# Fox-GLA encoder block on one core: six of sixteen k blocks of the first projection group multiplied as whole fp32 products

## Chip, cores and metric

One core of a Trainium2 chip runs the whole program. The metric is the device time in microseconds; lower is better. All tensors are float32. The kernel gets more accuracy out of TensorE than its fast fp32r format has by splitting each operand into a high part (the value rounded to fp32r) and a low part (what is left), and adding three products.

## The reference, cut to what matters

One layer with a token mixer and an MLP. Only its first part bears on this change: the shift and the scale of the first normalisation come from the conditioning vector `c` through `w_ada`, and the modulated `h` is multiplied by the columns of `w_in`.

```
mod = (c_act @ w_ada[i] + b_ada[i])[:, None, :]
shift_m, scale_m, gate_m, shift_f, scale_f, gate_f = jnp.split(mod, N_MOD, axis=-1)
h = rmsnorm(x, g_pre_mix[i]) * (1.0 + scale_m) + shift_m
...
proj = h @ w_in
fq, fk, fv, ff, gq, gk, gv, ga, gr = jnp.split(proj, IN_OFFSETS, axis=-1)
...
x = x + gate_m * rmsnorm(y, g_post_mix[i])
h = rmsnorm(x, g_pre_mlp[i]) * (1.0 + scale_f) + shift_f
y = squared_relu_mlp(h, w_mlp_in[i], w_mlp_out[i])
```

`x` is 512 x 2048, `w_ada` 2048 x 12288 and `w_in` 2048 x 6168.

## The kernel before

**Stages.** After a start (rows of `x` normalised, transposed into `xn_t`) the projection runs in eight groups of six 128-column tiles (`group_steps`, from L743), the first four for the attention heads and the last four for the linear-attention heads; the work of the heads of group r is threaded between the products of group r+1. Then follow the output projection, the MLP's input products and the MLP's output products. This change touches the first group (r = 0, `first=True`) and no other.

**One group.** Its depth of 2048 is cut into KT = 16 k blocks of 128. Two k blocks make a weight unit (units 0 to 7 of 128 x 1536 elements, 768 KB), which lands in `w_raw`, is rounded by ScalarE into `w_hi` (`split_hi`, `first_hi`) and subtracted by VectorE into `w_lo` (`split_lo`, `first_lo`). There are two slots of each, by the unit's parity. For each k block TensorE makes 6 tiles x 3 products of 128 x 128 by 128 x 512 into six PSUM banks (`split_mm`, L731: high by high, high by low, low by high), all 16 k blocks adding into the same banks.

**The first group** differs from the others in that the moving operand isn't there yet. It is made k block by k block: ScalarE writes `in_tmp` = scale * xn_t + shift (L1271) and rounds it to `in_hi` (L1274), and VectorE subtracts to `in_lo` (`modulated_lo`, L1817). `in_lo` and `in_tmp` are the same bytes. The scale and shift of four k blocks (a "block" of the VectorE program; there are four, 0 to 3) come from eight items of `w_ada` of 1 MB each (`load_am`, items 0 to 31, four buffers): VectorE multiplies and adds each item's two halves into `am_acc` (`add_am`, L1800 and L1802), TensorE then sums over partitions by 16 tiny matmuls (`start_slot`, L922, in TensorE's queue ahead of the block's products), and VectorE makes the columns `mod_a`, `mod_b` (`mod_columns_m`, L1832 to L1835) for which ScalarE waits. TensorE's program also has 16 narrow steps (`misc_step`, 40 columns of weights `wm_raw`, split in the same way), put at k blocks 5 to 15 by `MISC_AT`: k 5 to 9 have two each (steps 0, 1; 2, 3; 4, 5; 6, 7; 8, 9), k 10 to 15 have one.

**VectorE's order** for block b: mod columns; `w_lo` of unit 2b; `in_lo` of k 4b and 4b+1; (blocks 1 and 2) `wm_lo`; items; `w_lo` of unit 2b+1; `in_lo` of k 4b+2; one item; `in_lo` of k 4b+3; more items. In all these are nine items in block 0 (8 to 16), eight in block 1 (17 to 24), seven in block 2 (25 to 31) and none in block 3.

**SyncE's queue** issues all these transfers in one order: items in sequence, each when the item four before it has been used (`am_used`); small transfers of `wm_raw` behind items 9 to 24; unit 2 behind item 13, unit 3 behind item 17, unit 4 behind 21, unit 5 behind 25, unit 6 behind 29 and unit 7 behind 31. A unit of weights waits until the unit two before it has been split by both engines (`slot_free`, L473).

Of the kernel before, what the change touches and what calls it, by code (L numbers as in the profile page):

```python
# [45 lines left out]
def build_block(nc, x, c, w_ada, b_ada, g_pre_mix, g_post_mix, w_in, b_fgate, w_gla_a2, b_gla_a2,  # L46
# [64 lines left out]
    with ExitStack() as ctx:  # L111
# [261 lines left out]
        o_rstd = sem("o_rstd")  # L373
        o_ready = sem("o_ready")

        def arrived_group(r, mm):
            return 16 * GROUP_DMAS * (r * (MM_G // 2) + mm // 2 + 1)

# [90 lines left out]
        def _(sp):  # L469
# [2 lines left out]
                sp.wait_ge(hi_done, m - 1)  # L472
                sp.wait_ge(lo_done, m - 1)  # L473

            def load_fox(r, mm, wait=True):
                if wait:
                    slot_free(r * MM_G + mm)
                dst = group_view(w_raw[mm % 2])
                for k in range(2):
                    src = w_in_t[:, 2 * mm + k, 0:3 * FOX_WIDTH].rearrange("p (s n) -> p s n", s=3)  # L480
                    to = dst[:, k, :].rearrange("p (s n) -> p s n", s=3)
                    for part in (slice(0, 2), slice(2, 3)):
                        sp.dma_start(to[:, part, :], src[:, part, bass.ds(r * 2 * P, 2 * P)])\
                            .then_inc(w_in_s[mm % 2], 16)
# [109 lines left out]
            for n in range(9, 32):  # L594
                load_am(n)
                if n < 25:
                    load_wm(n - 9)
                if n == 25:
                    sp.dma_start(b_fg[32:40, :], b_fgate.rearrange("o h -> h o")).then_inc(bfg_in, 16)
                if n >= 13 and n % 4 == 1:  # L600
                    load_fox(0, (n - 5) // 4)
            load_fox(0, MM_G - 1)


            def load_cumb(f):
# [124 lines left out]
        def _(pe):  # L730
            def split_mm(dst, a, b, start, stop, onto=False):  # L731

                pe.matmul(dst, a[0], b[0], start=start, stop=False, skip_group_check=onto)  # L733
                pe.matmul(dst, a[0], b[1], start=False, stop=False, skip_group_check=onto)  # L734
                return pe.matmul(dst, a[1], b[0], start=False, stop=stop, skip_group_check=onto)  # L735

            def group_steps(r, first, slot, misc_step=None):

                for k in range(KT):
                    s, m = (k // 2) % 2, r * MM_G + k // 2  # L740
                    hi, lo = group_view(w_hi[s])[:, k % 2, :], group_view(w_lo[s])[:, k % 2, :]
                    if first:
                        slot(2 * k)  # L743
                    if k % 2 == 0:
                        pe.wait_ge(hi_done, m + 1)
                        pe.wait_ge(lo_done, m + 1)
                    if first:
                        pe.wait_ge(mod_lo, k + 1)
                        for n in MISC_AT[k]:
                            misc_step(n)  # L750
                    for b in range(TILES):
                        if k == 0 and not first:

                            pe.wait_ge((ev_act, ev_dve)[b % 2], r * 3 - 2 + b // 2)
                        cols = slice(b * P, b * P + P)
                        last = split_mm(bank[b][:, :], (hi[:, cols], lo[:, cols]),
                                        (in_hi[:, k, :], in_lo[:, k, :]), k == 0, k == KT - 1)
                        if k == KT - 1 and b < TILES - 1:
                            last.then_inc(tile_sum, 1)
                        if b == TILES - 1 and k % 2:  # L760
                            last.then_inc(w_used, 1)
                        if not first and b == 2:
                            slot(2 * k)
                    if not first:
                        slot(2 * k + 1)
# [161 lines left out]
            def misc_step(k):  # L927

                if k % 8 == 0:
                    pe.wait_ge(wm_hid, k // 8 + 1)  # L930
                    pe.wait_ge(wm_lod, k // 8 + 1)
                last = split_mm(BB[0:40, :], (wm_hi[:, k, :], wm_lo[:, k, :]), (in_hi[:, k, :], in_lo[:, k, :]),
                                k == 0, k == KT - 1)
                if k == KT - 1:
                    last.then_inc(misc_sum, 1)

# [2 lines left out]
            def fox_slots(f):  # L939
                def slot(s):  # L940
                    fox_slot(s, f)
                    if s == 30:
                        pe.wait_ge(fox_max, 8 * f + 8)
                        f_columns(f)
                return slot


            def first_fox_slot(s):
                if s == 0:
                    pe.wait_ge(cum_ready, 1)  # L950
                    for t in range(TB):
                        last = pe.transpose(BA[:, t * FOX_HEADS:(t + 1) * FOX_HEADS],
                                            f_z[32:40, t * P:t * P + P], ident[32:40, 32:40])
                    last.then_inc(cumq_tr, 1)
                if s == 1:
                    pe.wait_ge(cumq_ready, 1)
                fox_slots(0)(s)

            group_steps(1, False, first_fox_slot)
# [167 lines left out]
        def _(act):  # L1127
            def split_hi(m, arrived, n, view=slice(0, 2048)):

                act.wait_ge(w_in_s[n], arrived)  # L1130
                act.wait_ge(w_used, m - 1)
                act.activation(w_hi[n][:, view], w_raw[n][:, view], ACT.Copy).then_inc(hi_done, 1)  # L1132
# [132 lines left out]
            def first_hi(m):  # L1265
                act.wait_ge(w_in_s[m], arrived_group(0, m))
                act.activation(w_hi[m][:, NARROW], w_raw[m][:, NARROW], ACT.Copy).then_inc(hi_done, 1)
# [9 lines left out]
            for k in range(KT):  # L1277
                if k in (4, 8):
                    part = slice(2 * k - 8, 2 * k)
                    act.wait_ge(wm_in[k // 4 - 1], 256)  # L1280
                    act.activation(wm_hi[:, part, :], wm_raw[:, part, :], ACT.Copy).then_inc(wm_hid, 1)
                modulate(k)
                if k == 1:
                    first_hi(1)
                if k % 2 and 3 <= k < KT - 1:
                    mm = (k + 1) // 2
                    split_hi(mm, arrived_group(0, mm), mm % 2, NARROW)

            split_hi(MM_G, arrived_group(1, 0), 0, NARROW)
            act.wait_ge(fz_abs, 1)  # L1290
# [264 lines left out]
        def _(dve):  # L1555
# [259 lines left out]
            def modulated_lo(k, n):  # L1815
                dve.wait_ge(mod_hi, n + 1)
                dve.tensor_tensor(in_lo[:, k, :], in_tmp[:, k, :], in_hi[:, k, :].bitcast(F32),  # L1817
                                  ALU.subtract).then_inc(mod_lo, 1)

            def first_lo(m):  # L1820
                dve.wait_ge(hi_done, m + 1)
                dve.tensor_tensor(w_lo[m][:, NARROW], w_raw[m][:, NARROW], w_hi[m][:, NARROW].bitcast(F32),
                                  ALU.subtract).then_inc(lo_done, 1)

            def mod_columns_m(block):
                k = slice(4 * block, 4 * block + 4)

# [8 lines left out]

            for n in range(2, 8):
                add_am(n)
            for block in range(KT // 4):
                mod_columns_m(block)  # L1840
                if block == 0:
                    first_lo(0)
                else:
                    split_lo(2 * block, 0, NARROW)
                n = 8 * block + 8
                more = block < KT // 4 - 1
                modulated_lo(4 * block, 4 * block)
                modulated_lo(4 * block + 1, 4 * block + 1)
                if block == 0:
                    add_am(n)  # L1850
                if block in (1, 2):
                    part = slice(8 * block - 8, 8 * block)
                    dve.wait_ge(wm_hid, block)
                    dve.tensor_tensor(wm_lo[:, part, :], wm_raw[:, part, :], wm_hi[:, part, :].bitcast(F32), ALU.subtract)\
                        .then_inc(wm_lod, 1)
                if more:
                    add_am(n + 1)
                    add_am(n + 2)
                if block == 0:
                    first_lo(1)  # L1860
                else:
                    split_lo(2 * block + 1, 1, NARROW)
                modulated_lo(4 * block + 2, 4 * block + 2)
                if more:
                    add_am(n + 3)
                modulated_lo(4 * block + 3, 4 * block + 3)
                if more:
                    for i in range(4, 9 if block < KT // 4 - 2 else 8):
                        add_am(n + i)
            dve.wait_ge(am_used, 32)  # L1870

            split_lo(MM_G, 0, NARROW)
            dve.wait_ge(misc_sum, 1)
# [487 lines left out]
```

## Time and profile before

| what | value |
| --- | --- |
| median of 3 runs | 2239.73 us (2239.48 to 2239.76) |
| time of the profiled execution | 2241.82 us |
| its span in the trace | 2240.0 us |
| mean granted TensorE clock | 0.989 |
| TensorE busy | 2163.1 us, 97% of the span |
| first group's products in the trace | 44.93 to 154.94 us |

The span is the time from the first to the last instruction. The profiled execution took 1.82 us more than its span and 2.09 us more than the median of the runs. The first group is 5% of the span. PE is TensorE's matmuls, PEld its weight loads, DVE is VectorE, ACT ScalarE, POOL GpSimd and SP SyncE. A matmul's duration in a row reaches past the start of the next, because matmuls are pipelined; what one costs is read from start to start. In the trace's rows a split product's two kinds are named by L733, L734 and L735.

### The profile page before, as it was taken

How to read it: one execution, taken by the hardware profiler on the slowest of the kernel's cores; microseconds unless marked ns; L12 is line 12 of the kernel's file. 1: busy time of each engine (PE TensorE's matmuls, PEld its weight loads, DVE VectorE, ACT ScalarE, POOL GpSimd, SP SyncE). 2: the span in 40 equal slices, each digit the busy share in tenths (PEclk: the TensorE clock that was granted, in tenths of full speed). 3: DMA queues.
4: the chain of work that ended last, by engine and by line, in shares of the span. 5: the costliest groups of instructions: out<-in, count | busy, mean ns of one | idle time of the engine just before them, and what ended most of it. 6: DMA issues, size and time to landing. Idle time of an engine off the chain costs nothing.

```text
span 2240.0 us, 26539 instructions
## 1 busy us (share of the span) xinstructions
PE 2163.1 (97%) x9847; PEld 1769.0 (79%) x9847; DVE 1510.3 (67%) x1467; ACT 868.8 (39%) x1094; POOL 379.2 (17%) x209
## 2 busy tenths in 40 slices
PE   4799999999999999999999999999999999999996
PEld 3577888887777788888888888888878888888885
DVE  6967666666767634655445544543698989898998
ACT  6333333331334223534334335334444444343443
POOL 1000000000000000100000000000034545463645
PEclk9899999999999999999999999999999999999998
DMA  9946555653553352566656646756355664567663
GB/s 366 347 158 228 189 172 165 226 156 101 185 164 116 112 214 76 192 221 225 202 194 217 223 170 205 246 183 202 132 196 179 239 232 166 191 232 245 236 232 143
DMA packets 262306, 441.16 MB, mean 197 GB/s; under 512 B 18156, under 2 KB 110512, under 8 KB 256184
## 3 DMA queue, kind: packets, MB, share of 16 engines
q1 hardware_dynamic: 261376, 435.45, 57.8%
q10 hardware_dynamic: 824, 4.27, 0.5%
q8 instruction: 70, 1.15, 0.2%
q14 instruction: 36, 0.29, 0.0%
HBM read 379.88 MB, written 59.79 MB: 196 GB/s over the span
## 4 chain that ended last, share of the span: by engine, by line
PE 78%; issue 8%; DVE 6%; DMA 2%; ACT 1%; DVEq 1%; POOL 1%; SPq 1%; POOLq 0%; ACTq 0%
PE pair L733 25%; PE pair L735 25%; PE pair L734 25%; DVE am_acc L1800 3%; DMA w_raw<-in_w_in 1%; PE pair L830 1%; DMA am_item<-in_w_ada 1%; DVE v_op L2067 1%; PE pair L804 1%; DVEq L1799 1%; POOL v_raw L2319 0%; PE pair L922 0%; PE pair L870 0%; PE pair L821 0%; PE pair L879 0%
## 5 line engine op out<-in xcount | busy, mean ns | idle before, releaser
L733 PE MATMUL pair<-in_hi,w_hi 128*128 128x512 f32 (+1 forms) x1824 | 730.1, 400 | 12.0 <-DVE in_lo L1817 6.5
L735 PE MATMUL pair<-in_hi,w_lo 128*128 128x512 f32 (+1 forms) x1824 | 707.3, 388 | 0.0
L734 PE MATMUL pair<-in_lo,w_hi 128*128 128x512 f32 (+1 forms) x1824 | 706.3, 387 | 0.0
L1560 DVE TENSOR_TENSOR w_lo<-w_raw,w_hi 128x2048 fp32r<-128x2048 f32 (+1 forms) x142 | 294.7, 2075 | 407.2 <-ACT w_hi L1132 406.7
L1132 ACT ACTIVATE w_hi<-w_raw 128x2048 fp32r<-128x2048 f32 (+1 forms) x142 | 244.9, 1725 | 466.3 <-PE pair L735 416.6
L733 PEld LDWEIGHTS pair<-in_hi,w_hi 128*128 128x128 f32 x1824 | 344.6, 189 | 92.1 <-issue 22.1
L735 PEld LDWEIGHTS pair<-in_hi,w_lo 128*128 128x128 f32 x1824 | 343.8, 188 | 71.6
L734 PEld LDWEIGHTS pair<-in_lo,w_hi 128*128 128x128 f32 x1824 | 345.0, 189 | 69.0 <-issue 2.6
L733 PE MATMUL pair<-v_op,hid_r 128*128 128x512 f32 x896 | 349.1, 390 | 2.1 <-issue 0.8
L735 PE MATMUL pair<-v_op,hid_r 128*128 128x512 f32 x896 | 348.6, 389 | 0.0
L734 PE MATMUL pair<-v_op,hid_r 128*128 128x512 f32 x896 | 348.6, 389 | 0.0
L2067 DVE TENSOR_TENSOR v_op<-v_raw,v_op 128x1024 fp32r<-128x1024 f32 x192 | 302.3, 1595 | 64.6 <-ACT v_op L1537 63.5
L1537 ACT ACTIVATE v_op<-v_raw 128x1024 fp32r<-128x1024 f32 x192 | 203.3, 1061 | 287.0 <-PE pair L735 269.0
L2310 POOL TENSOR_TENSOR v_sum<-v_raw,v_raw 128x512 f32<-128x512 f32 x60 | 149.2, 2515 | 363.3 <-DVE v_raw L2082 363.3
L733 PEld LDWEIGHTS pair<-v_op,hid_r 128*128 128x128 f32 x896 | 168.2, 188 | 39.0 <-issue 3.2
L735 PEld LDWEIGHTS pair<-v_op,hid_r 128*128 128x128 f32 x896 | 168.2, 188 | 35.0
L734 PEld LDWEIGHTS pair<-v_op,hid_r 128*128 128x128 f32 x896 | 168.2, 188 | 34.7
L2319 POOL TENSOR_TENSOR v_raw<-v_raw,v_sum 128x512 f32<-128x512 f32 x60 | 135.4, 2288 | 18.4 <-DVE v_op L2067 18.4
L2237 POOL TENSOR_TENSOR ada<-ada,c_act 128x2048 f32<-128x2048 f32 x8 | 30.4, 3804 | 592.3 <-DMA ada<-in_w_ada 555.0
L2117 DVE TENSOR_TENSOR y_t<-pair,y_t 128x1024 f32<-128x1024 f32 x104 | 124.9, 1214 | 0.3 <-PE pair L735 0.3
L733 PE MATMUL pair<-w_hi,in_hi 128*128 128x512 f32 x256 | 101.2, 395 | 0.0
L734 PE MATMUL pair<-w_lo,in_hi 128*128 128x512 f32 x256 | 99.7, 389 | 0.0
(205 smaller groups left out, 1886.0 us busy)
## 6 DMA issues: line engine op xcount, KB each, us to landing
w_raw<-in_w_mlp_in SPq DMA_DIRECT2D x64, 1024.0 KB, 5.3
v_raw<-in_w_mlp_out SPq DMA_DIRECT2D x128, 512.0 KB, 5.0
hid_r<-hid_scratch SPq DMA_DIRECT2D x112, 512.0 KB, 6.2
hid_scratch<-hid_r SPq DMA_DIRECT2D x28, 1792.0 KB, 8.3
am_item<-in_w_ada SPq DMA_DIRECT2D x64, 512.0 KB, 7.2
w_raw<-in_w_in SPq DMA_DIRECT2D x128, 256.0 KB, 3.6
af_item<-in_w_ada SPq DMA_DIRECT2D x64, 512.0 KB, 4.5
w_raw<-in_w_in SPq DMA_DIRECT2D x128, 128.0 KB, 3.6
```

What stands on the lines that cost most here:

```text
L733: pe.matmul(dst, a[0], b[0], start=start, stop=False, skip_group_check=onto)
L734: pe.matmul(dst, a[0], b[1], start=False, stop=False, skip_group_check=onto)
L735: return pe.matmul(dst, a[1], b[0], start=False, stop=stop, skip_group_check=onto)
L1132: act.activation(w_hi[n][:, view], w_raw[n][:, view], ACT.Copy).then_inc(hi_done, 1)
L1537: act.activation(v_op[i % 4][:, 0, :], raw_of(u, p)[:, h, :], ACT.Copy).then_inc(v_hi, 1)
L1560: dve.tensor_tensor(w_lo[n][:, view], w_raw[n][:, view], w_hi[n][:, view].bitcast(F32), ALU.subtract)\
L1800: last = dve.scalar_tensor_tensor(total, item, c_k, total, ALU.mult, ALU.add)
L2067: dve.tensor_tensor(v_op[i % 4][:, 1, :], raw_of(u, p)[:, h, :], v_op[i % 4][:, 0, :].bitcast(F32), ALU.subtract).then_inc(v_lo, 1)
L2117: return dve.tensor_tensor(dst, src[:, :, :], dst, ALU.add)
L2237: pool.tensor_tensor(unit[:, :, :], unit[:, :, :], c_act[:, :].rearrange("p (k o) -> p k o", o=1).to_broadcast([P, KT, P]), ALU.mult)\
L2310: last = pool.tensor_tensor(v_sum[:, h, cols], v_raw[q[B22]][:, h, cols], v_raw[q[B11]][:, h, cols], ALU.add)
L2319: last = pool.tensor_tensor(b21, b21, v_sum[:, h, cols], ALU.subtract)
```

## The change

For the weight units 1, 3 and 5 of the first group (k blocks 2, 3, 6, 7, 10 and 11), TensorE multiplies `w_raw` by `in_tmp` in one fp32 `pe.matmul` per tile instead of three products of parts; the same holds for the narrow steps of those k numbers (`wm_raw` by `in_tmp`). These units are split neither by ScalarE nor by VectorE. TensorE waits for the arrival of the raw unit and for `mod_tmp` instead of for the splits. As `in_lo` overwrites `in_tmp`, VectorE makes the `in_lo` of these six k blocks after the items are done and after unit 5 has been used (`w_used` of 6). A transfer into a slot whose last unit was a whole one waits for TensorE's use of that unit: unit 3 for unit 1, unit 5 for unit 3, unit 7 for unit 5. The counts of `hi_done` and `lo_done` are made up by 3 when unit 6 is split.

```diff
--- before.py
+++ after.py
@@ -373,6 +373,16 @@
         o_rstd = sem("o_rstd")
         o_ready = sem("o_ready")
 
+        WHOLE = (1, 3, 5)
+
+        def whole(k):
+            return k // 2 in WHOLE
+
+        LO_ORDER = [k for k in range(KT) if not whole(k)] + [k for k in range(KT) if whole(k)]
+
+        def splits(m):
+            return m + 1 if m > max(WHOLE) else sum(u not in WHOLE for u in range(m + 1))
+
         def arrived_group(r, mm):
             return 16 * GROUP_DMAS * (r * (MM_G // 2) + mm // 2 + 1)
 
@@ -472,8 +482,13 @@
                 sp.wait_ge(hi_done, m - 1)
                 sp.wait_ge(lo_done, m - 1)
 
-            def load_fox(r, mm, wait=True):
-                if wait:
+            def load_fox(r, mm, wait=True, first=False):
+                if wait and first and mm - 2 in WHOLE:
+                    sp.wait_ge(w_used, mm - 1)
+                elif wait and first:
+                    sp.wait_ge(hi_done, splits(mm - 2))
+                    sp.wait_ge(lo_done, splits(mm - 2))
+                elif wait:
                     slot_free(r * MM_G + mm)
                 dst = group_view(w_raw[mm % 2])
                 for k in range(2):
@@ -598,8 +613,8 @@
                 if n == 25:
                     sp.dma_start(b_fg[32:40, :], b_fgate.rearrange("o h -> h o")).then_inc(bfg_in, 16)
                 if n >= 13 and n % 4 == 1:
-                    load_fox(0, (n - 5) // 4)
-            load_fox(0, MM_G - 1)
+                    load_fox(0, (n - 5) // 4, first=True)
+            load_fox(0, MM_G - 1, first=True)
 
 
             def load_cumb(f):
@@ -741,11 +756,18 @@
                     hi, lo = group_view(w_hi[s])[:, k % 2, :], group_view(w_lo[s])[:, k % 2, :]
                     if first:
                         slot(2 * k)
-                    if k % 2 == 0:
-                        pe.wait_ge(hi_done, m + 1)
-                        pe.wait_ge(lo_done, m + 1)
+                    raw = group_view(w_raw[s])[:, k % 2, :]
+                    by_parts = not (first and whole(k))
+                    if k % 2 == 0 and not by_parts:
+                        pe.wait_ge(w_in_s[s], arrived_group(0, m))
+                    elif k % 2 == 0:
+                        pe.wait_ge(hi_done, splits(m) if first else m + 1)
+                        pe.wait_ge(lo_done, splits(m) if first else m + 1)
                     if first:
-                        pe.wait_ge(mod_lo, k + 1)
+                        if by_parts:
+                            pe.wait_ge(mod_lo, LO_ORDER.index(k) + 1)
+                        else:
+                            pe.wait_ge(mod_tmp, k + 1)
                         for n in MISC_AT[k]:
                             misc_step(n)
                     for b in range(TILES):
@@ -753,8 +775,11 @@
 
                             pe.wait_ge((ev_act, ev_dve)[b % 2], r * 3 - 2 + b // 2)
                         cols = slice(b * P, b * P + P)
-                        last = split_mm(bank[b][:, :], (hi[:, cols], lo[:, cols]),
-                                        (in_hi[:, k, :], in_lo[:, k, :]), k == 0, k == KT - 1)
+                        if by_parts:
+                            last = split_mm(bank[b][:, :], (hi[:, cols], lo[:, cols]),
+                                            (in_hi[:, k, :], in_lo[:, k, :]), k == 0, k == KT - 1)
+                        else:
+                            last = pe.matmul(bank[b][:, :], raw[:, cols], in_tmp[:, k, :], start=False, stop=False)
                         if k == KT - 1 and b < TILES - 1:
                             last.then_inc(tile_sum, 1)
                         if b == TILES - 1 and k % 2:
@@ -929,8 +954,11 @@
                 if k % 8 == 0:
                     pe.wait_ge(wm_hid, k // 8 + 1)
                     pe.wait_ge(wm_lod, k // 8 + 1)
-                last = split_mm(BB[0:40, :], (wm_hi[:, k, :], wm_lo[:, k, :]), (in_hi[:, k, :], in_lo[:, k, :]),
-                                k == 0, k == KT - 1)
+                if whole(k):
+                    last = pe.matmul(BB[0:40, :], wm_raw[:, k, :], in_tmp[:, k, :], start=False, stop=False)
+                else:
+                    last = split_mm(BB[0:40, :], (wm_hi[:, k, :], wm_lo[:, k, :]), (in_hi[:, k, :], in_lo[:, k, :]),
+                                    k == 0, k == KT - 1)
                 if k == KT - 1:
                     last.then_inc(misc_sum, 1)
 
@@ -954,6 +982,7 @@
                     last.then_inc(cumq_tr, 1)
                 if s == 1:
                     pe.wait_ge(cumq_ready, 1)
+                    pe.wait_ge(mod_lo, KT)
                 fox_slots(0)(s)
 
             group_steps(1, False, first_fox_slot)
@@ -1280,11 +1309,11 @@
                     act.wait_ge(wm_in[k // 4 - 1], 256)
                     act.activation(wm_hi[:, part, :], wm_raw[:, part, :], ACT.Copy).then_inc(wm_hid, 1)
                 modulate(k)
-                if k == 1:
-                    first_hi(1)
-                if k % 2 and 3 <= k < KT - 1:
-                    mm = (k + 1) // 2
+                mm = (k + 1) // 2
+                if k % 2 and 3 <= k < KT - 1 and mm not in WHOLE:
                     split_hi(mm, arrived_group(0, mm), mm % 2, NARROW)
+                    if mm == max(WHOLE) + 1:
+                        act.sem_inc(hi_done, len(WHOLE))
 
             split_hi(MM_G, arrived_group(1, 0), 0, NARROW)
             act.wait_ge(fz_abs, 1)
@@ -1817,11 +1846,6 @@
                 dve.tensor_tensor(in_lo[:, k, :], in_tmp[:, k, :], in_hi[:, k, :].bitcast(F32),
                                   ALU.subtract).then_inc(mod_lo, 1)
 
-            def first_lo(m):
-                dve.wait_ge(hi_done, m + 1)
-                dve.tensor_tensor(w_lo[m][:, NARROW], w_raw[m][:, NARROW], w_hi[m][:, NARROW].bitcast(F32),
-                                  ALU.subtract).then_inc(lo_done, 1)
-
             def mod_columns_m(block):
                 k = slice(4 * block, 4 * block + 4)
 
@@ -1836,12 +1860,18 @@
 
             for n in range(2, 8):
                 add_am(n)
+            def lo_first(m):
+                dve.wait_ge(hi_done, splits(m))
+                dve.tensor_tensor(w_lo[m % 2][:, NARROW], w_raw[m % 2][:, NARROW], w_hi[m % 2][:, NARROW].bitcast(F32),
+                                  ALU.subtract).then_inc(lo_done, 1)
+                if m == max(WHOLE) + 1:
+                    dve.sem_inc(lo_done, len(WHOLE))
+
             for block in range(KT // 4):
                 mod_columns_m(block)
-                if block == 0:
-                    first_lo(0)
-                else:
-                    split_lo(2 * block, 0, NARROW)
+                if block:
+                    dve.wait_ge(w_used, 2 * block - 1)
+                lo_first(2 * block)
                 n = 8 * block + 8
                 more = block < KT // 4 - 1
                 modulated_lo(4 * block, 4 * block)
@@ -1856,18 +1886,19 @@
                 if more:
                     add_am(n + 1)
                     add_am(n + 2)
-                if block == 0:
-                    first_lo(1)
+                if not more:
+                    split_lo(2 * block + 1, 1, NARROW)
+                    modulated_lo(4 * block + 2, 4 * block + 2)
+                    modulated_lo(4 * block + 3, 4 * block + 3)
                 else:
-                    split_lo(2 * block + 1, 1, NARROW)
-                modulated_lo(4 * block + 2, 4 * block + 2)
-                if more:
                     add_am(n + 3)
-                modulated_lo(4 * block + 3, 4 * block + 3)
                 if more:
                     for i in range(4, 9 if block < KT // 4 - 2 else 8):
                         add_am(n + i)
             dve.wait_ge(am_used, 32)
+            dve.wait_ge(w_used, max(WHOLE) + 1)
+            for k in LO_ORDER[-2 * len(WHOLE):]:
+                modulated_lo(k, k)
 
             split_lo(MM_G, 0, NARROW)
             dve.wait_ge(misc_sum, 1)
```

## Rows read from the trace of the kernel before

**Rows 1.** The page, first part: busy time, share and instructions of each engine.
```profile
PE 2163.1 (97%) x9847; PEld 1769.0 (79%) x9847; DVE 1510.3 (67%) x1467; ACT 868.8 (39%) x1094; POOL 379.2 (17%) x209
```

**Rows 2.** Windows by stage, first group; PE: stretch, length, busy, clock, DMA share, GB/s.
```profile
44.93:64.48 19.55, 18.89 (x72) 0.89 1.08 369
64.48:70.23 5.75, 0.00 (x0) 0.95 1.07 364
...
76.76:98.96 22.20, 22.20 (x90) 0.93 0.99 327
...
105.30:128.37 23.07, 23.07 (x90) 0.88 0.83 289
128.37:133.83 5.46, 2.10 (x17) 0.75 0.00 0
133.83:154.94 21.11, 21.11 (x84) 0.90 0.39 125
```

**Rows 3.** Waits from 40 to 160 us: in total, times, the longest.
```profile
PE pair L733 <- DVE in_lo L1817: 12.4, 5, 3.0
...
PE pair L922 <- DVE am_acc L1800: 7.4, 3, 5.8
```

**Rows 4.** Timeline, VectorE, first block and the start of the second: start, length.
```profile
53.52 1.75 DVE L1822 TENSOR_TENSOR w_lo<-w_raw,w_hi 128x1536 fp32r<-128x1536 f32 x1
...
58.54 0.69 DVE L1817 TENSOR_TENSOR in_lo<-in_tmp,in_hi 128x512 fp32r<-128x512 f32 x1
59.32 10.86 DVE L1800 SCALAR_TENSOR_TENSOR am_acc<-am_item,c_act,am_acc 128x1024 f32<-128x1024 f32 x8
70.09 0.74 DVE L1802 TENSOR_SCALAR am_acc<-am_item,c_act 128x1024 f32<-128x1024 f32 x1
70.91 1.28 DVE L1800 SCALAR_TENSOR_TENSOR am_acc<-am_item,c_act,am_acc 128x1024 f32<-128x1024 f32 x1
73.84 0.16 DVE L1832 TENSOR_TENSOR mod_b<-pair,cols_a 128x4 f32<-128x4 f32 x1 [1.64 <-PE pair L922]
```

**Rows 5.** Timeline, TensorE: an fp32 product of a later group between split ones.
```profile
189.25 1.02 PE L804 MATMUL pair<-grp 128*128 128x512 f32 x2
...
190.34 0.40 PE L734 MATMUL pair<-in_lo,w_hi 128*128 128x512 f32 x1
```

**Rows 6.** Timeline, TensorE: the first rows of two stretches that lie 18 products apart.
```profile
119.47 0.39 PE L733 MATMUL pair<-in_hi,w_hi 128*128 128x512 f32 x1
...
123.55 0.39 PE L733 MATMUL pair<-in_hi,wm_hi 128*40 128x512 f32 x1
```

**Rows 7.** Timeline, TensorE: the column sums ahead of the second, third and fourth block.
```profile
70.23 3.57 PE L922 MATMUL pair<-ones,am_acc 128*128 128x1 f32 x16 [5.76 <-DVE am_acc L1800]
...
100.40 1.95 PE L922 MATMUL pair<-ones,am_acc 128*128 128x1 f32 x16 [1.28 <-DVE am_acc L1800]
...
128.93 1.95 PE L922 MATMUL pair<-ones,am_acc 128*128 128x1 f32 x16 [0.41 <-DVE am_acc L1800]
```

**Rows 8.** Windows of all engines: stretch, length, busy of five engines, clock, DMA share, GB/s.
```profile
44.00:64.00 20.00, 18.42 (x71) 14.84 (x72) 18.44 (x18) 6.90 (x9) 0.00 (x0) 0.87 1.08 369
...
80.00:82.00 2.00, 2.00 (x11) 1.60 (x10) 1.91 (x2) 1.27 (x2) 0.00 (x0) 1.00 0.53 170
```

**Rows 9.** The tile am_item, the two transfers issued at 58.6 us: from issue to landing.
```profile
L570 SPq DMA_DIRECT2D am_item<-in_w_ada x2: 379/426/472, 58.6 to 59.1; - x2
...
DMA to landing us min/median/max: 5.7/6.5/7.3
```

**Rows 10.** Timeline, SyncE's queue: when transfers were issued.
```profile
66.72 2.22 SPq L483 DMA_DIRECT2D w_raw<-in_w_in  x4
...
94.90 0.89 SPq L570 DMA_DIRECT2D am_item<-in_w_ada  x2
...
96.34 1.94 SPq L483 DMA_DIRECT2D w_raw<-in_w_in  x4
98.33 12.16 SPq L570 DMA_DIRECT2D am_item<-in_w_ada  x8
```

## What the change is predicted to do

> **What bounds the kernel now.** I read the page first: TensorE is busy for 97% of the span [rows 1], so nearly all the rest of the program moves one for one with the moment at which the first group ends. The question is the first group alone. The windows by stage [rows 2] show it as four blocks of TensorE work with gaps: 44.93 to 64.48, 76.76 to 98.96, 105.30 to 128.37 and 133.83 to 154.94 us. The first gap is 12.3 us long, the second 6.3, the third 5.5. The waits say who ends them: VectorE's item sums ahead of the column sums, 7.4 us in all, and then `in_lo`, 12.4 us in five waits [rows 3]. Four of these five are the fixed turnaround behind the column sums, about 2.95 us each: mod columns, one `w_lo`, one `in_lo`. From the start of warm column sums to the first product it is 105.30 - 100.40 = 4.90 and 133.83 - 128.93 = 4.90 us [rows 2, 7]. Outside that turnaround TensorE waited 5.75 us for VectorE ahead of block 1 (64.48 to 70.23), about 1.4 ahead of block 2 (98.96 to 100.40) and about 0.5 ahead of block 3 (128.37 to 128.93). That is the reader's main point: **VectorE leads the first gap only; in the other two TensorE follows it by about one microsecond**.
>
> **VectorE.** The change takes from each of blocks 0, 1 and 2 one `w_lo` and two `in_lo` [rows 4]. A `w_lo` shows 1.75 us and an `in_lo` 0.69; from start to start they are a little shorter (58.54 to 59.32 with the drain is 0.78, a `w_lo` about 1.67). So 1.67 + 0.69 + 0.78 = 3.15 us a block, 9.4 in all. The six `in_lo` come back behind the items, 6 x 0.69 = 4.1 us, in block 3. There VectorE has only two `w_lo` and four `in_lo` to make, some 6 us, while TensorE computes for 21.1 us [rows 2]; they are first read in group 1. I cost them at nothing; without that cover they would cost 4.1 us.
>
> **TensorE.** Three split products come one after another each 0.227 us: 18 of them lie in 123.55 - 119.47 = 4.08 us [rows 6]. So a split step is 0.68 us. The nearest row for an fp32 product of the same shape is L804 in a later group: it is recorded as two instructions, starts at 189.25, and the second split product behind it starts at 190.34; less one split product of 0.23 that leaves 0.86 us [rows 5]. A whole step thus costs 0.18 us more. That price isn't shown for a long row of such products. The bound below is two instructions at a split product's pace, 0.45; the one above is the 1.02 us that the row shows for the pair. I take 0.86, as it is a reading from start to start of this very operation. How many steps: 12 tiles in each of blocks 0, 1, 2, and narrow steps 2 and 3 (k 6), 6 and 7 (k 8), 10 and 11. Block 0 gains 12 x 0.18 = 2.1 us of work, block 1 14 x 0.18 = 2.5, block 2 16 x 0.18 = 2.85; 7.5 us in all. In block 0 the wait of about 1 us for `in_lo` and `w_lo` inside the block goes away, so block 0 ends at 64.5 + 2.1 - 1.0 = 65.5.
>
> The Trainium skill's page "TensorE: Matmul & The Clock Gate", section "Wait — 56ns, not 53.3ns?", gives 215.7 ns from one warm 512-column matmul to the next, and "FP8 and Floating Point Precision", section "TensorE Precision Notes", gives true fp32 four passes. By these pages a whole step would be 0.86 us and a split one 0.65, the 42 steps would cost 9.1 us and the result would be 1.2 us later than mine. The trace's 0.227 [rows 6] decides, since it is this kernel's own.
>
> **Block 1's start.** Does VectorE's 3.15 us arrive? The transfers say: not all. From 44 to 64 us the DMA engines are full (share 1.08, 369 GB/s) [rows 8], so what must land by a given moment is fixed by bytes, not by when it is asked for. The item whose last sum ends block 0's demand (item 15) was issued at 58.65 and 59.1 us, its last half landed 7.3 us later, at 66.4 [rows 9]. VectorE began it at about 67.5 and was done at 70.18 [rows 4]. So it can be done at 66.4 + 2.73 = 69.1 at the earliest: **1.05 us of gain, not 3.15**. Item 16 (0.74 + 1.28) stands before the mod columns as now. The column sums were slow here, 3.57 us against 1.95 [rows 7], nearly twice as long, as at 1.2 instead of 2.4 GHz; the clock of the gap ahead of them is 0.95 on the mean [rows 2], so it fell late in it. With a shorter idle (65.5 to 69.2) it may be granted longer, for up to 1.6 us more; I don't count on it. Block 1 starts at 76.76 - 1.05 = 75.7.
>
> **From there TensorE leads.** Block 1: 22.20 + 2.5 = 24.7 us, to 100.4. VectorE needs to be ready for block 2 by then: it starts its items 1.05 us earlier and has no `w_lo` and `in_lo` between them, so its last sum, now at 100.2, comes at about 96.2. Column sums and turnaround 4.9: block 2 starts at 105.3, as before. Block 2: 23.07 + 2.85 = 25.9, to 131.2. Again 4.9 and some 0.1: block 3 starts at 136.2 against 133.83. Block 3 has no whole step. **The first group ends 2.3 us later.** Its pieces against before: +5.35 of work in blocks 1 and 2, -1.05 at block 1's start, -1.9 of waits for VectorE used up (1.4 and 0.5).
>
> **SyncE's queue.** The new waits on `w_used` stand in one queue with the items. Unit 3 now waits for the end of block 0 (65.5), which is earlier than it was issued (66.72) [rows 10], and nothing is late. Unit 5 waits for the end of block 1, 100.4, where it was issued at 96.34; behind it are items 26 to 31. Item 26 was issued at 98.33 and is now at 102.3. Items 24 and 25 are ahead of the stall. VectorE uses item 25 at 106.6 to 109.3 and then one each 2.73 us, item 28 lands about 112.5 (three items of 1.05 MB at 369 GB/s, 2.85 us each, behind the unit), so the last sum comes at about 125.7, and TensorE asks for it at 131.2: 5.5 us of cover. Unit 7 waits for 131.2 instead of 118; it lands by about 136.5, and is first wanted by TensorE at about 148. ScalarE loses three roundings of 1.5 us, off the path.
>
> **Sum.** The profiled execution took 2241.82 us; by this it becomes 2244.1. The median stood 2.09 us below it, so the median becomes 2239.73 + 2.3 = 2242.0. About 0.2% (4.5 us) is what a measurement of this kernel can tell from no change, so this counts as none.
>
> **Rivals.**
> 1. *VectorE's full gain reaches block 1.* If the transfers give way, block 1 starts at 72.0 (3.15 us from VectorE, 1.6 from warm column sums). Then 96.7, 101.6, 127.5, 132.4: 1.4 us faster, 2238.3. Against it: a share of 1.08 [rows 8] and only 0.53 once VectorE had let the queue run dry. The Trainium skill's "DMA: Bandwidth & Descriptors", section "Bandwidth", states 425 GB/s for large loads where the row has 369; by that rate this rival would hold. Chance 0.12.
> 2. *Whole steps are cheap* (a run of them overlaps so that each costs no more than a split step's 0.68). Then only the transfers and VectorE count: blocks 1, 2 and 3 keep their gain, 1.05, then 3.15 more each at best less the 1.4 and 0.5 us that TensorE has to give. 1.05 + 1.4 + 0.5 = 3 us; with full gain at block 1 as in the first rival 6.6 us faster, 2233 to 2236.7. Against it: two instructions of 0.43 in L804's row [rows 5]. Chance 0.06.
> 3. *Slower: whole steps are dear.* A run of fp32 products costs more than a lone one, up to the pair's 1.02 us. 42 x 0.34 = 14.3 us of work instead of 7.5, of which block 0's hides in the gap: 30 x 0.16 = 4.8 on top of 2.3, 2246.8. It passes 0.2% from 0.93 us a step on. For it: nobody has shown twelve in a row; against it: weight loads of 0.19 us fit under 0.43. Chance 0.09.
> 4. *Slower: unit 5's wait starves VectorE.* It decides once item 31's sum is over 5.5 us later than I find; beyond that each microsecond counts, and 2244.5 to 2248 would come out. Chance 0.05.
> Each block also starts at 1.2 GHz: mean clock 0.93 in block 1 and 0.88 in block 2 [rows 2], so, at half the clock, stretches of (1 - 0.93) x 2 x 22.2 = 3.1 and 5.5 us, worth 1.2 us between the best and the worst in each block. That was hidden by VectorE before and isn't now.
>
> **Numbers.** My case has 0.68. The range takes in the first rival and product prices to 0.92: 2238.0 to 2245.0. Faster by over 0.2% is the second rival's upper part, 0.05; slower is rivals 3 and 4 with the unlucky end of my own case, 0.15; the same 0.80.
>
> **What the changed profile would show.** Whole products as pairs 0.86 us apart; block 0 ending at 65.5; column sums ahead of block 1 at 69.1; no wait of L922 for `am_acc` ahead of blocks 2 and 3, with VectorE idle before the mod columns; block 2 starting at 105.3, block 3 at 136.2. I am wrong if L922 still waits for VectorE ahead of block 2, if block 1 starts before 74 us, or if whole steps aren't within 0.85 to 0.9.

## The result, and the profile after

The changed kernel takes 2243.89 us (median of 22 runs, 2241.24 to 2245.94) against 2240.06 us for the kernel before in the same series (22 runs). The ratio is 1.0015, 95% interval 1.0009 to 1.0021: 3.4 us slower, 2.0 to 4.7 (the two medians lie 3.8 us apart). The forecast was 2242.0 us, 2.3 slower, in a range of 2238.0 to 2245.0. The measured time lies in that range and the loss is below the 4.5 us that the forecast took for the least it could tell, but it is clear of zero. The profiled execution took 2243.09 us with a span of 2241.2 us.

Windows by stage of the changed kernel, first group; the columns are those of [rows 2]:

```profile
45.03:65.69 20.66, 20.66 (x60) 0.90 1.08 369
65.69:68.81 3.12, 0.01 (x1) 1.00 1.07 362
...
74.65:100.40 25.75, 25.75 (x76) 0.90 0.95 327
...
105.29:131.95 26.66, 26.66 (x74) 0.90 0.73 264
131.95:136.81 4.86, 1.90 (x17) 0.76 0.56 162
136.81:158.11 21.30, 21.30 (x84) 0.89 0.39 124
```

Blocks 1 and 2 are longer than in [rows 2], by 3.6 us each; block 3, which has no whole step, is not. The wait ahead of block 1 has shrunk from 5.75 us to 3.12.

From the start of group 1 to the end the two profiled executions took 2083.4 us (before) and 2081.4 (changed); over all twelve profiles of this document it is 2081.1 to 2083.4. So single profiles show where the first group's time goes, but a difference of one or two microseconds in the whole is read from the medians: group 1 starts 3.2 us later here, while the two spans differ by only 1.2.

Waits of the changed kernel from 40 to 160 us, beside [rows 3]:

```profile
DVE mod_b L1856 <- PE pair L947: 13.0, 4, 5.6
...
DVE am_acc L1829 <- DMA am_item<-in_w_ada: 5.3, 6, 2.3
...
PE pair L947 <- DVE am_acc L1829: 3.1, 1, 3.1
```

The roles have turned. TensorE waits for the item sums once, ahead of block 1, instead of three times. VectorE waits 13.0 us for TensorE's column sums (7.2 before), and 5.3 us for the transfers, which it did not wait for in this stretch before.

Timeline of the changed kernel, TensorE, the column sums and whole steps up to block 2 (start, length), beside [rows 7]:

```profile
68.81 2.88 PE L947 MATMUL pair<-ones,am_acc 128*128 128x1 f32 x16 [3.12 <-DVE am_acc L1829]
74.65 0.77 PE L748 MATMUL pair<-in_hi,w_hi 128*128 128x512 f32 x1 [2.96 <-DVE in_lo L1846]
...
88.69 5.42 PE L782 MATMUL pair<-in_tmp,w_raw 128*128 128x512 f32 x12
...
95.34 5.32 PE L782 MATMUL pair<-in_tmp,w_raw 128*128 128x512 f32 x12
100.49 1.73 PE L947 MATMUL pair<-ones,am_acc 128*128 128x1 f32 x15
```

A row x12 is one k block: six products, recorded as two instructions each. From 95.34 to the sums at 100.49 it is 5.15 us for six, 0.86 us each. Block 0's twelve lie between 55.23 and 65.69, 0.87 each. Ahead of the sums at 100.49 there is no idle time.

Timeline of the changed kernel, VectorE: the item sums of block 0 and of block 2, beside [rows 4]:

```profile
54.23 8.13 DVE L1829 SCALAR_TENSOR_TENSOR am_acc<-am_item,c_act,am_acc 128x1024 f32<-128x1024 f32 x6 [0.52 <-issue]
63.26 2.64 DVE L1829 SCALAR_TENSOR_TENSOR am_acc<-am_item,c_act,am_acc 128x1024 f32<-128x1024 f32 x2 [0.90 <-DMA am_item<-in_w_ada]
66.12 2.64 DVE L1829 SCALAR_TENSOR_TENSOR am_acc<-am_item,c_act,am_acc 128x1024 f32<-128x1024 f32 x2 [0.21 <-DMA am_item<-in_w_ada]
...
109.74 10.86 DVE L1829 SCALAR_TENSOR_TENSOR am_acc<-am_item,c_act,am_acc 128x1024 f32<-128x1024 f32 x8 [0.16 <-DMA am_item<-in_w_ada]
122.90 5.38 DVE L1829 SCALAR_TENSOR_TENSOR am_acc<-am_item,c_act,am_acc 128x1024 f32<-128x1024 f32 x4 [2.31 <-DMA am_item<-in_w_ada]
133.89 0.16 DVE L1856 TENSOR_TENSOR mod_b<-pair,cols_a 128x4 f32<-128x4 f32 x1 [5.61 <-PE pair L947]
```

Items 14 and 15 (63.26, 66.12) are each begun when they land. In block 2 item 30 is begun when it lands, at 122.9, with item 31 right behind it. They are late, but VectorE ends them at 128.3, 3.7 us before TensorE ends block 2 (131.95). Its wait of 5.6 us is these 3.7 and the column sums.

Timeline of the changed kernel, SyncE's queue, the stall of unit 5, beside [rows 10]:

```profile
90.14 1.30 SPq L585 DMA_DIRECT2D am_item<-in_w_ada  x2
91.48 0.42 SPq L614 DMA_DIRECT2D b_fg<-in_b_fgate  x1
100.69 1.88 SPq L498 DMA_DIRECT2D w_raw<-in_w_in  x4
102.61 7.88 SPq L585 DMA_DIRECT2D am_item<-in_w_ada  x8
```

For 9 us nothing is issued. The forecast had unit 5 at 100.4 and item 26 at 102.3.

### The profile page after: what moved, and what is told of

Its sections match the earlier page's. It is cut to its first block, busy times and chain, and to the rows that moved or that the text cites. A ratio compares the mean times of both kernels' runs of the same rounds, so it can differ in the third digit from the quotient of the medians.

```text
span 2241.2 us, 26445 instructions
## 1 busy us (share of the span) xinstructions
PE 2170.7 (97%) x9805; PEld 1761.1 (79%) x9805; DVE 1506.4 (67%) x1464; ACT 864.9 (39%) x1091; POOL 378.4 (17%) x209
## 4 chain that ended last, share of the span: by engine, by line
PE 83%; issue 8%; DVE 3%; DMA 2%; POOL 1%; SPq 1%; ACT 1%; POOLq 0%; DVEq 0%; ACTq 0%
PE pair L748 26%; PE pair L750 26%; PE pair L749 26%; DMA am_item<-in_w_ada 1%; DVE am_acc L1829 1%; PE pair L782 1%; PE pair L855 1%; PE pair L829 1%; DVE v_op L2098 1%; PE pair L947 0%; DMA w_raw<-in_w_in 0%; POOL v_raw L2350 0%; PE pair L846 0%; PE pair L895 0%; PE pair L904 0%
## 5 line engine op out<-in xcount | busy, mean ns | idle before, releaser
L748 PE MATMUL pair<-in_hi,w_hi 128*128 128x512 f32 (+1 forms) x1788 | 716.2, 401 | 11.4 <-DVE in_lo L1846 5.9
L750 PE MATMUL pair<-in_hi,w_lo 128*128 128x512 f32 (+1 forms) x1788 | 693.4, 388 | 0.0
L749 PE MATMUL pair<-in_lo,w_hi 128*128 128x512 f32 (+1 forms) x1788 | 692.6, 387 | 0.0
L1589 DVE TENSOR_TENSOR w_lo<-w_raw,w_hi 128x2048 fp32r<-128x2048 f32 (+1 forms) x137 | 286.0, 2088 | 401.2 <-ACT w_hi L1161 400.6
L748 PEld LDWEIGHTS pair<-in_hi,w_hi 128*128 128x128 f32 x1788 | 337.9, 189 | 91.0 <-issue 22.5
L750 PEld LDWEIGHTS pair<-in_hi,w_lo 128*128 128x128 f32 x1788 | 337.2, 189 | 70.1
L749 PEld LDWEIGHTS pair<-in_lo,w_hi 128*128 128x128 f32 x1788 | 338.2, 189 | 67.5 <-issue 2.6
```

Source lines behind the costliest of these rows:

```text
L1589: dve.tensor_tensor(w_lo[n][:, view], w_raw[n][:, view], w_hi[n][:, view].bitcast(F32), ALU.subtract)\
```

## Experiments

All were run in five rounds beside the kernel before. The table holds, from each profile, the length of the column sums ahead of block 0, the start of those ahead of block 1, the starts of blocks 1, 2 and 3 and of group 1 (us), and the ratio of the times to the kernel before.

| kernel | sums 0, length | sums 1 | block 1 | block 2 | block 3 | group 1 | ratio (95% interval) |
| --- | --- | --- | --- | --- | --- | --- | --- |
| before | 3.31 | 70.23 | 76.76 | 105.30 | 133.83 | 156.63 | 1 |
| changed | 3.39 | 68.81 | 74.65 | 105.29 | 136.81 | 159.79 | 1.0015 (1.0009 to 1.0021) |
| unit 1 only | 3.46 | 69.03 | 75.27 | 103.82 | 132.35 | 155.70 | 0.9999 (0.9990 to 1.0008) |
| units 1, 3 | 2.20 | 69.00 | 75.52 | 106.43 | 134.96 | 157.86 | 1.0004 (0.9995 to 1.0013) |
| units 3, 5 | 2.98 | 69.85 | 76.38 | 105.78 | 137.24 | 160.19 | 1.0021 (1.0012 to 1.0030) |
| half columns | 1.92 | 69.36 | 75.89 | 102.78 | 129.14 | 152.28 | 0.9984 (0.9975 to 0.9993) |
| unit 5 later | 1.92 | 69.15 | 75.68 | 105.61 | 136.75 | 159.24 | 1.0018 (1.0009 to 1.0027) |
| unit 2 later | 1.92 | 66.79 | 73.44 | 104.09 | 135.57 | 158.52 | 1.0012 (1.0003 to 1.0021) |
| unit 1 only, unit 2 later | 1.92 | 66.85 | 73.47 | 102.08 | 131.65 | 154.88 | 0.9991 (0.9982 to 1.0000) |
| the same again | 1.92 | 66.76 | 73.38 | 102.33 | 131.56 | 155.12 | 0.9990 (0.9981 to 0.9999) |
| unit 1 only, unit 2 at 15 | 1.92 | 66.82 | 74.17 | 102.71 | 131.24 | 154.84 | 0.9996 (0.9987 to 1.0005) |
| before, unit 2 later | 1.92 | 69.10 | 75.64 | 104.18 | 132.73 | 155.42 | 1.0001 (0.9992 to 1.0010) |

**1. Only unit 1 whole.**

```diff
-        WHOLE = (1, 3, 5)
+        WHOLE = (1,)
```

with `split_lo` and the two `modulated_lo` back in the VectorE program for units not in `WHOLE`.

> Only unit 1 (block 0) is multiplied whole; units 3 and 5 are split again, with their in_lo in the old places. Theory (TensorE leads from block 1 on, so whole steps there are pure cost, and block 0's are hidden by the wait for the items): block 1 starts at 74.6 us as in the changed kernel, then VectorE leads again at its old pace: block 2 at 103.2, block 3 at 131.7, each 2.1 us earlier than before the change; the time 2.1 us below before, 5 us below the changed kernel. Rival (the new waits in SyncE's queue, not TensorE's work, cost the time): unit 3's wait is still there, so part of the loss stays and block 2 starts at 105 or later.

Blocks 2 and 3 start at 103.82 and 132.35: 1.5 us before the kernel before and 4.5 before the changed one at block 3. The rival, 105 or later at block 2, fell. These are the sums ahead of blocks 2 and 3 in the timeline of TensorE:

```profile
98.92 1.95 PE L947 MATMUL pair<-ones,am_acc 128*128 128x1 f32 x16
...
127.45 1.95 PE L947 MATMUL pair<-ones,am_acc 128*128 128x1 f32 x16 [1.44 <-DVE am_acc L1829]
```

Ahead of block 3 TensorE waits 1.44 us for VectorE again. Ahead of block 2 neither waits: VectorE's last sum ends at 98.86 and TensorE's last product at 98.88. The loss is gone, so it sits in units 3 and 5. But the expected 2.1 us of gain is not in the profile (1.5 us at blocks 2 and 3, 0.9 at group 1), and the time (between 2.2 us less and 1.8 more) can't tell 0.9 us from none. That part of the theory missed; see below.

**2. Units 1 and 3 whole** (`WHOLE = (1, 3)`).

> Units 1 and 3 are whole, unit 5 is split. Theory: blocks 0 and 1 as in the changed kernel (74.65, 105.3), block 2 back to about 23.5 us of TensorE work, 128.8. But the items behind unit 5's wait come late, and VectorE has 3.1 us of splits between them again, so it may lead: block 3 starts between 133.8 and 135.5 against 136.8 in the changed kernel; the time 0 to 1.7 us above before. Rival (whole steps cost nothing and the waits do): block 3 still at 136.8.

Block 3 at 134.96, inside what was expected, and the time 0.9 us above before (between 1.1 less and 2.9 more). Blocks 1 and 2 started 0.9 and 1.1 us later than expected. From the start of block 1 to that of block 3 it is 57.1 us with unit 1 alone, 59.4 here and 62.2 in the changed kernel: each of the two later units adds its part. VectorE did not lead again: the sums ahead of block 3 began at 130.17 without a wait.

**3. Units 3 and 5 whole** (`WHOLE = (3, 5)`, and `first_hi(1)` back in ScalarE's program).

> Units 3 and 5 whole, unit 1 split as before the change: the part of the change that the theory calls pure cost, alone. Theory: block 1 starts at 76.8 us as before, block 2 at 106.5 to 107.3, block 3 at 138 to 139, group 1 at 161 to 162, 4 to 5 us later than before; the time 4 to 5.5 us above before, above the changed kernel too. Rival (the parts share one gain on VectorE): block 2 no later than 105.3.

2.7 to 6.7 us slower than before. The marks are 0.4 to 0.8 us earlier than the expected ranges and block 2 came only 0.5 us behind the rival's 105.3, but the direction holds: without the gain at block 1 the two later units alone put group 1 at 160.19, later than all three do (159.79). The times of this kernel and of the changed one can't be told apart.

**4. Half the columns of the wide whole products.**

```diff
-                            last = pe.matmul(bank[b][:, :], raw[:, cols], in_tmp[:, k, :], start=False, stop=False)
+                            last = pe.matmul(bank[b][:, 0:256], raw[:, cols], in_tmp[:, k, 0:256], start=False, stop=False)
```

> The changed kernel with the second half of the columns left out of the 36 wide whole products (256 of 512), waits and order unchanged. Theory: a wide whole step costs 0.44 us instead of 0.87, 5.2 us less in each of blocks 0, 1 and 2. Block 1 starts at 74.65 unchanged; block 2 at about 101.8 (VectorE's items end at 96.9), block 3 at about 128; the time 8 to 9 us below the changed kernel, about 5 below before. Rival (TensorE's work doesn't lead): block 2 still at 105.3 and the time within 1 us of the changed kernel.

Windows of this kernel, TensorE, block 2 (21.12 us, where the changed kernel's has 26.66):

```profile
102.78:123.90 21.12, 21.11 (x74) 0.91 0.83 300
```

and its timeline, the sums that follow:

```profile
97.68 1.95 PE L947 MATMUL pair<-ones,am_acc 128*128 128x1 f32 x16 [1.66 <-DVE am_acc L1829]
...
124.23 1.95 PE L947 MATMUL pair<-ones,am_acc 128*128 128x1 f32 x16 [0.34 <-DVE am_acc L1829]
```

With about 5.5 us less work in a block, TensorE waits for VectorE again and block 3 starts 7.7 us before the changed kernel's; block 1's start is not earlier. TensorE's work is what led there. The gain stops where VectorE takes over, about 1 us sooner than expected: the time is 3.6 us below before (1.6 to 5.6) where about 5 was expected.

**5. Unit 5's load later in SyncE's queue.**

```diff
-                if n >= 13 and n % 4 == 1:
+                if n >= 13 and n % 4 == 1 and n != 25:
                     load_fox(0, (n - 5) // 4, first=True)
+                if n == 28:
+                    load_fox(0, 5, first=True)
```

> The changed kernel with unit 5's load put behind item 28 instead of item 25, so that its wait for w_used holds back no item that could go earlier. Theory (the stall in SyncE's queue is covered): items 26 to 28 are issued before 100 us, VectorE ends its items at 126 instead of 128.3 us, TensorE's blocks stay at 105.3 and 136.8, the time within 0.7 us of the changed kernel. Rival (the stall costs): block 3 starts 1 to 2 us earlier, and so the time.

Its VectorE sums all of block 2's items without a break, and then waits 1.9 us longer for TensorE than in the changed kernel (5.61):

```profile
107.26 19.07 DVE L1831 SCALAR_TENSOR_TENSOR am_acc<-am_item,c_act,am_acc 128x1024 f32<-128x1024 f32 x14
133.84 0.16 DVE L1858 TENSOR_TENSOR mod_b<-pair,cols_a 128x4 f32<-128x4 f32 x1 [7.51 <-PE pair L949]
```

Block 3 starts at 136.75 against 136.81. The stall in the queue costs nothing here.

**6. Unit 2's load behind item 16.**

```diff
-                if n >= 13 and n % 4 == 1:
+                if n >= 17 and n % 4 == 1:
                     load_fox(0, (n - 5) // 4, first=True)
+                if n == 16:
+                    load_fox(0, 2, first=True)
```

> The changed kernel with unit 2's load (768 KB, 2.1 us of the engines' time) put behind item 16 instead of item 13, where it is no longer ahead of items 14 and 15. Theory (full transfer engines, not VectorE, set when block 1 starts; in all four kernels run so far the column sums ahead of it began between 68.8 and 69.4 us, wherever block 0 began): VectorE no longer waits for items 14 and 15, the column sums begin at 67.6 to 68.0, and as TensorE leads from there the whole group ends 0.5 to 1.3 us earlier than in the changed kernel. Rival (VectorE sets it): still 68.8 or later.

The sums ahead of block 1 begin at 66.79, even earlier than expected. Timeline of this kernel, VectorE: ten item sums, those of items 14 and 15 among them, without a wait, and then a new one:

```profile
53.14 13.60 DVE L1831 SCALAR_TENSOR_TENSOR am_acc<-am_item,c_act,am_acc 128x1024 f32<-128x1024 f32 x10 [0.65 <-DMA am_item<-in_w_ada]
66.97 0.75 DVE L1833 TENSOR_SCALAR am_acc<-am_item,c_act 128x1024 f32<-128x1024 f32 x1 [0.23 <-DMA am_item<-in_w_ada]
...
70.94 1.76 DVE L1867 TENSOR_TENSOR w_lo<-w_raw,w_hi 128x1536 fp32r<-128x1536 f32 x1 [1.39 <-ACT w_hi L1163]
```

Unit 2 now comes late for its own split (1.39 us), so block 1 gains about 2.2 us on experiment 5's and not 3.6. Group 1 starts 0.7 us before experiment 5's and 1.3 before the changed kernel's. The time (0.7 to 4.7 us above before) can't be told from the changed kernel's.

**7. Unit 1 whole and unit 2 behind item 16**, edits 1 and 6 together, run twice.

> Only unit 1 whole, and unit 2's load behind item 16: the two places where the runs say that the change gives something. Theory: column sums ahead of block 1 at 67.6 to 68.0 us, block 2 at 102.5 to 102.9, block 3 at 131.0 to 131.4, 2.5 us earlier than before the change; group 1 starts at about 154.3 against 156.6; the time 1.5 to 2.5 us below before. Rival (the gain is lost in the later transfers): block 3 at 132.3 as with unit 1 alone.

> Only unit 1 whole and unit 2's load behind item 16, the same kernel again, to narrow its interval. Both theories: 1.5 to 2.5 us below before.

2237.72 and 2237.88 us where the kernel before had 2239.3 and 2239.74: 1.6 and 1.9 us less by the medians, 2.0 and 2.2 by the ratios 0.9991 and 0.9990, the first interval ending at 1 and the second just clear of it. Block 2 came at 102.1 and 102.3, earlier than expected, block 3 at 131.65 and 131.56 and group 1 at 154.9 and 155.1, a little later. This version is clearly faster than the changed kernel, and faster than the kernel before by a margin that two series agree on and that is hardly wider than their intervals.

**8. The same with unit 2 behind item 15** (`n == 15`).

> Only unit 1 whole, unit 2's load behind item 15. Unit 2 no longer holds up the first w_lo of block 1 (1.4 us in the version behind item 16), but item 16 lands 2.1 us later and is summed ahead of the mod columns. Theory: column sums at 66.8, mod columns at about 71.2, block 1 at 74.1 against 73.5: group 1 starts 0.3 to 0.8 us later than with unit 2 behind item 16, the time between the two versions. Rival (the late unit was the dearer of the two): block 1 at 72.5 or earlier.

Block 1 at 74.17 as expected, 0.7 us later than in 7. Group 1 starts no later (154.84 against 154.88 and 155.12) where 0.3 to 0.8 us later was expected, and the times (0.9996) can't be told apart from 7.

**9. The kernel before with unit 2 behind item 16.**

> The kernel before the change, with unit 2's load behind item 16 instead of item 13, and nothing whole. Theory (two resources lead to block 1's start one behind the other: VectorE first, the transfers 1.1 us behind): without whole steps VectorE isn't ahead of the transfers, so the earlier items bring nothing; column sums ahead of block 1 at 70.2 us, group 1 at 156.4 to 157.0, the time within 0.7 us of before. Rival (the transfers alone led): column sums at 68 or earlier and the time 1 to 2 us below before.

No change that the times show (between 1.8 us less and 2.2 more). The sums began at 69.10 and group 1 at 155.42, both 1.1 to 1.2 us before the kernel before and earlier than expected. But VectorE's only wait for a transfer was 0.37 us at 49.85; from there it went through its work without a break. Block 0 had begun 1.4 us earlier too, at 43.53 (next section). So the earlier marks don't come from the moved load: VectorE leads until its work is cut.

## Why the forecast was right, and where it was off

**Block 0's end and the price.** Forecast 65.5, measured 65.69; a wide whole step 0.86 forecast, 0.86 to 0.87 measured. Right.

**Where it was off: the work of blocks 1 and 2.** They took 25.75 and 26.66 us, forecast 24.7 and 25.9: 1.8 us more in all. In block 1 it is the clock. Windows of TensorE, the kernel before and then two of the changed one:

```profile
70.00:79.50 9.50, 6.32 (x23) 0.50 1.08 367
...
70.00:79.50 9.50, 6.54 (x20) 0.50 1.08 367
80.00:82.00 2.00, 2.00 (x11) 1.00 1.05 344
```

In both kernels the clock was at half (1.2 GHz) from 70.00 to 79.50 and full from 80.00 on, though block 1 started at 76.76 in one and at 74.65 in the other. The 2.1 us by which it started earlier lie wholly in the slow stretch and hold only about 1.05 us of work, and 1.05 is what block 1 took beyond the forecast.

In block 2 the clock says nothing against the forecast (0.90 against 0.88). There it is the narrow steps, which the forecast had priced as wide ones. Timeline of the kernel before, and then of the changed one:

```profile
118.78 0.40 PE L733 MATMUL pair<-in_hi,wm_hi 128*40 128x512 f32 x1
...
86.84 1.91 PE L958 MATMUL pair<-in_tmp,wm_raw 128*40 128x512 f32 x4
119.44 1.05 PE L958 MATMUL pair<-in_tmp,wm_raw 128*40 128x512 f32 x2
120.43 5.42 PE L782 MATMUL pair<-in_tmp,w_raw 128*128 128x512 f32 x12
```

Two narrow whole steps at full clock took 1.85 us from start to start (86.84 to 88.69), and one between wide ones 0.99 (119.44 to 120.43), not 0.86. The k blocks 10 and 11 took 12.5 us (119.44 to 131.95) against 9.6 before (118.78 to 128.37): 2.9 for 14 steps where the forecast had 2.5. The two narrow whole steps at the start of block 2 ran at 1.2 GHz and took 3.60 us against 2.54 for the split ones before.

**TensorE leads from block 1 on.** Shown: no wait for the items ahead of blocks 2 and 3, block 3 4.5 us earlier when units 3 and 5 are split again, 7.7 us earlier when the products are halved. Block 2 was forecast at 105.3 and started at 105.29. That this fits to 0.01 us is luck: block 1 started 1.05 us earlier than forecast and took 1.05 us longer. Block 3 was forecast at 136.2 and started at 136.81.

**The transfers hold block 1's start.** Shown: in the five kernels whose unit 1 is whole and unit 2 is in its old place, the sums ahead of block 1 began at 68.81 to 69.36 us, wherever block 0 began; with unit 2 out of the way they began at 66.8. The forecast had 69.1.

**Where it was off: the 1.05 us of gain at block 1.** In the profiled executions block 1 started 2.1 us earlier than before: 1.4 us from the start of the column sums (68.81 against 70.23), and 0.7 because the sums themselves were quicker (2.88 us against 3.57), which the forecast had left out. But 1.05 us was 69.1 compared with the 70.18 of one profiled execution, and this starting point moves. The length of the very first column sums differs from execution to execution, 1.92 us or up to 3.46, with the clock that TensorE is granted there, and VectorE waits for them:

```profile
38.72 3.39 PE L947 MATMUL pair<-ones,am_acc 128*128 128x1 f32 x16 [1.87 <-DVE am_acc L1829]
```

is the changed kernel's, and this is experiment 9's:

```profile
38.70 1.92 PE L924 MATMUL pair<-ones,am_acc 128*128 128x1 f32 x16 [2.52 <-DVE am_acc L1802]
```

Where these sums are quick, VectorE without the change is ready at 69.10 (experiment 9), and with it the transfers allow no less (69.15 in experiment 5); block 1 starts at 75.64 and 75.68. By these two the gain is then nothing, though each of them has one load moved, and the two kernels themselves were not profiled in the quick case. Seven of the ten experiments had the quick case; the profile of before, on which I built, had the slow one. Experiment 9's group 1 starts at 155.42, experiment 5's at 159.24: 3.8 us between split and whole units when both begin quickly, 3.2 between the two kernels when both begin slowly. The measured 3.4 lies between, but its interval (2.0 to 4.7) holds both, and the forecast 2.3 too, so the times don't decide.

So the terms of the sum that were mis-sized are two. The work of blocks 1 and 2 was forecast at +5.35 us and was 6.1 in the quick pair (experiments 5 and 9) and 7.1 in the slow one. The gain at block 1, forecast at 1.05, was nothing in the quick pair and 2.1 in the slow one, of which half was lost to the slow clock. The waits for VectorE that were used up, 1.9, were right. Experiment 1 began slowly, like the kernel before, and still gained only 1.5 us at blocks 2 and 3 where 2.1 was expected: its block 1 started at 75.27, not at 74.6, with sums of 3.28 us, not 2.88. How often either case occurs in the timed runs was not measured.

**Rivals.** The first (VectorE's full gain) fell: even with unit 2 moved, block 1 started at 73.4, not 72.0. The full transfer engines moved 362 to 369 GB/s ahead of block 1 in the changed kernel, as before. The second and third (whole steps cheap or dear) fell with 0.87 us. The fourth (unit 5's wait) was real in the queue: VectorE waited 2.3 us for item 30 and ended item 31 at 128.3, where the forecast had 125.7. 3.7 us of cover were left of the 5.5 in the forecast; experiment 5 shows that it costs nothing. By the Trainium skill's page "TensorE: Matmul & The Clock Gate", section "Wait — 56ns, not 53.3ns?", split products should have been 215.7 ns apart; the trace kept its 0.227, and with it the sum.

## What to carry to other kernels

Work handed to an engine that waits pays only up to that engine's idle time in the same stage (here block 0 had 5.75 us for 2.1 us of extra work, blocks 1 and 2 had 1.9 us for 5.35 by the forecast and 7.1 in the profile), so read the idle time stage by stage and change only the stage that has it. When an engine is relieved, look next at what lands just ahead of its use: here the full transfer engines took the gain back until a weight unit that nobody needed yet was moved behind the items. And before a term of one microsecond is read from one execution, ask whether its starting point moves with the clock.

## What the runs showed of the hardware beyond what was expected

- The 16 one-column products ahead of block 0 took 1.92 us in seven of the ten experiments, and 2.20, 2.98 and 3.46 in the others; 3.31 and 3.39 in the two kernels compared. The same code at the same moment finds the clock at either level: the granted clock over these products was 1.00 in the seven and 0.51 to 0.84 in the other five. In the seven TensorE had stood idle for 2.1 to 2.5 us before them, in the five for 1.2 to 1.9. Why is not shown.
- Fp32 products of 128 x 128 by 128 x 512 in a row cost 0.86 to 0.87 us each, no less than a lone one. With 40 columns of weights instead of 128 they cost not less but more, 0.92 us for each of two and 0.99 between wide ones; at 1.2 GHz 1.8 us (two in 3.60).
- With the transfer engines full, item sums began at the pace of the landings, 2.86 us apart (63.26 to 66.12) for 1 MB and its small companions, against 2.69 of work (four items between 59.32 and 70.09 in [rows 4]).
